# Two more buffers for expert weight pieces in a two-layer hybrid trunk step

## The reference

```python
for each layer l:
    sh1, sc1, g1, sh2, sc2, g2 = split(silu(cond) @ w_ada[l] + b_ada[l], 6)
    h = rms_norm(x, norm1) * (1 + sc1) + sh1
    qa, ka, va, hy, qr, kr, vr, gr = split(h @ w_in[l])        # 1024 x 4608
    ya = diff_attention(...)                                    # branch A
    yb = hyena_mixer(hy, ...)                                   # branch B, long convolution
    yc = retention(...) * silu(gr)                              # branch C
    ga, gb, gc = split(sigmoid(h @ w_gate[l] + b_gate[l]), 3)   # 1024 x 3072
    merged = ga * (ya @ w_branch_a) + gb * (yb @ w_branch_b) + gc * (yc @ w_branch_c)
    x = x + g1 * (merged @ w_out[l])
    h2 = rms_norm(x, norm2) * (1 + sc2) + sh2
    # 16 experts in 4 groups, best group, best 2 experts in it, for every token
    a = einsum('bld,edf->blef', h2, moe_w1[l]); b = einsum('bld,edf->blef', h2, moe_w3[l])
    x = x + g2 * einsum('blef,efd->bld', silu(a) * b * gate, moe_w2[l])
y = rms_norm(x, final_g)
```

## Time and profile before

| | us |
|---|---|
| median of the three runs | 1155.75 |
| profiled execution, span from first to last instruction | 1155.5 |
| PE busy | 1100.4 (95%) |
| PE weight load busy | 783.7 (68%) |
| DVE busy | 542.0 (47%) |
| ACT busy | 209.8 (18%) |
| POOL busy | 41.0 (4%) |

### The profile page before, as it was taken

One profiled execution on the slowest core, in us unless ns is written; L12 is line 12 of the kernel. 1 busy time (PEld: TensorE's weight loads), 2 busy tenths in 40 slices (PEclk: granted clock), 3 DMA queues, 4 the chain that ended last, 5 costly groups with the idle time before them and its releaser, 6 DMA issues.

```text
span 1155.5 us, 15668 instructions
## 1 busy us (share of the span) xinstructions
PE 1100.4 (95%) x6026; PEld 783.7 (68%) x6026; DVE 542.0 (47%) x1202; ACT 209.8 (18%) x440; POOL 41.0 (4%) x83
## 2 busy tenths in 40 slices
PE   6999999999999999999889999999999999999965
PEld 4688888878887445454358888888888844545422
DVE  2469887677846311121244886646543551111003
ACT  3251022232021101111025111323201210000001
POOL 1001110000000000000000111000000000000000
PEclk9999999999998999999999999999999899999999
DMA  9657865467587999999955677437347979999993
GB/s 382 284 204 279 326 221 227 168 270 272 219 350 318 419 420 422 420 421 421 421 219 201 215 276 285 174 133 283 139 145 306 375 305 421 421 420 421 421 420 121
DMA packets 56943, 351.38 MB, mean 304 GB/s; under 512 B 7088, under 2 KB 7264, under 8 KB 20512
## 3 DMA queue, kind: packets, MB, share of 16 engines
q1 hardware_dynamic: 52704, 337.75, 73.5%
q0 software_dynamic: 4160, 12.58, 3.0%
HBM read 346.08 MB, written 2.65 MB: 302 GB/s over the span
## 4 chain that ended last, share of the span: by engine, by line
PE 84%; DMA 8%; DVE 3%; SPq 3%; ACT 1%; issue 1%; DVEq 0%; ACTq 0%
PE bank L836 26%; PE bank L1127 15%; PE bank L1016 7%; PE bank L1148 6%; DMA ring<-in_experts 5%; PE bank L1037 5%; PE bank L831 5%; PE bank L1112 5%; PE bank L1169 3%; PE bank L847 3%; DMA ring<-in_weights 3%; SPq L615 2%; PE bank L760 1%; PE bank L820 1%; PE bank L961 1%
## 5 line engine op out<-in xcount | busy, mean ns | idle before, releaser
L836 PE MATMUL bank<-h,ring 128*128 128x256 f32 x1472 | 324.8, 380 | 0.0
L836 PEld LDWEIGHTS bank<-h,ring 128*128 128x128 f32 x1472 | 277.4, 190 | 40.1 <-issue 3.2
L1750 DVE SCALAR_TENSOR_TENSOR ring<-ring 128x1024 f32<-128x1024 f32 x160 | 189.5, 1222 | 18.7 <-DMA ring<-in_mod_weights 9.1
L1127 PE MATMUL bank<-ring,gates 128*32 128x512 f32 (+2 forms) x616 | 137.7, 614 | 8.8 <-DMA h<-in_experts 5.0
L1127 PEld LDWEIGHTS bank<-ring,gates 128*32 128x32 f32 (+2 forms) x616 | 41.2, 126 | 69.5 <-issue 69.1
L1127 PE MATMUL bank<-lent,gates 128*32 128x512 f32 (+2 forms) x408 | 81.4, 593 | 2.0 <-ACTq L1618 2.0
L2238 DVE COPY uc_zt_dsum<-bank 128x512 f32<-128x512 f32 x14 | 9.7, 692 | 122.8 <-PE bank L1148 122.8
L1148 PE MATMUL bank<-ring,gates 128*32 128x512 f32 (+1 forms) x240 | 64.4, 595 | 2.0 <-issue 1.2
L1148 PE MATMUL bank<-lent,gates 128*32 128x512 f32 (+2 forms) x304 | 60.5, 594 | 1.3 <-DMA ring<-in_experts 1.0
L1112 PE MATMUL bank<-uc_zt_dsum,gates 128*128 128x128 f32 x448 | 55.5, 285 | 1.0 <-DVEq L2246 1.0
L1127 PEld LDWEIGHTS bank<-lent,gates 128*32 128x32 f32 (+2 forms) x408 | 25.2, 123 | 46.2 <-issue 43.7
(11 more groups left out here) (271 smaller groups left out, 1203.7 us busy)
## 6 DMA issues: line engine op xcount, KB each, us to landing
ring<-in_experts SPq DMA_DIRECT2D x93, 1024.0 KB, 19.8
ring<-in_weights SPq DMA_DIRECT2D x85, 1024.0 KB, 7.7
lent<-in_experts SPq DMA_DIRECT2D x72, 1024.0 KB, 17.8
ring<-in_mod_weights SPq DMA_DIRECT2D x80, 512.0 KB, 5.1
h<-in_experts SPq DMA_DIRECT2D x10, 1024.0 KB, 19.4
uc_zt_dsum<-in_experts SPq DMA_DIRECT2D x10, 1024.0 KB, 19.5
va_vr<-in_experts SPq DMA_DIRECT2D x7, 1024.0 KB, 12.2
lent<-in_weights SPq DMA_DIRECT2D x3, 1024.0 KB, 23.5
```

The lines of the kernel that those rows point to most:

```text
L836: last = pe.matmul(bank[b][:, c * TOK:(c + 1) * TOK], w[:, k, c * P:(c + 1) * P], h[:, k, :], start=(k == 0), stop=(k == KT - 1))
L1127: last = pe.matmul(bank[b][rows, :], hgat[:, 4 * half + f, rows], w[j][:, f, :], start=(half == 1 and f == 0), stop=(half == 0 and f == 3) ...
L1750: last = dve.scalar_tensor_tensor(out, w, 0.5, cond_wide[:, c, :], ALU.mult, ALU.mult, accum_out=mod_all[:, of, row, c:c + 1])
```

## The change

ring_table gets two more slots for expert pieces. EXTRA_SLOT is a new tile of 128 x 2048 (8 KB per partition) that only expert pieces use, so it is open at any time. SPARE_SLOT is a tile of the same size, open once the merge is done; rinv, rmsi and condT become parts of it. The room comes from the scratch of GpSimd's queue, which shrinks from 16384 to 4096 bytes per partition, 12 KB, and from the three small tiles (4 KB per partition together), for two tiles of 8 KB. As every slot has a semaphore of its own, two are added and three others are joined to ones that exist: s_hid_sum to s_taps_sum, s_hid_arg to s_taps, s_taps_abs to s_hid, with the counts waited for adapted. The wait for the turned tokens (line 613) is confined to the three slots that need it.

```diff
@@ -85,6 +85,7 @@
 LANDINGS = 3
 TOKENS_SLOT = SLOTS + LENT
 SUMS_SLOT, SHIFT_SLOT = TOKENS_SLOT + 1, TOKENS_SLOT + 2
+EXTRA_SLOT, SPARE_SLOT = SHIFT_SLOT + 1, SHIFT_SLOT + 2
 SHIFT_PIECES = 36
 OPENING_LENT = (SLOTS, SLOTS + 1, SLOTS + 2)
 
@@ -149,7 +150,7 @@
     pieces = [(item, c) for item in PLAN for c in range(PLAN_PIECES[item[0]])]
     done = [(item, c) for item in DONE for c in range(PLAN_PIECES[item[0]])]
     gone = {piece: n + 1 for n, piece in enumerate(done)}
-    free, filled = [0] * (SHIFT_SLOT + 1), [0] * (SHIFT_SLOT + 1)
+    free, filled = [0] * (SPARE_SLOT + 1), [0] * (SPARE_SLOT + 1)
     slot, count, used = [], [], []
     for (kind, layer, number), c in pieces:
         since = {at: free[at] for at in range(LEAST)}
@@ -158,6 +159,8 @@
         elif kind == "moe":
             since.update({at: max(free[at], END["merge", layer, 5]) for at in range(LEAST, SLOTS + LENT)})
         if kind == "moe":
+            since[EXTRA_SLOT] = free[EXTRA_SLOT]
+            since[SPARE_SLOT] = max(free[SPARE_SLOT], END["merge", layer, 5])
             for at in (TOKENS_SLOT, SUMS_SLOT):
                 since[at] = max(free[at], END["out", layer, N_PROJ - 1])
             if layer == DEPTH - 1 or c < SHIFT_PIECES:
@@ -360,9 +363,7 @@
         s_h_ready_s = sem("h_ready_s")
         s_h_ready_v = sem("h_ready_v")
         s_h_scaled = sem("h_scaled")
-        s_hid = sem("hid")
-        s_hid_arg = sem("hid_arg")
-        s_hid_sum = sem("hid_sum")
+        s_hid = sem("hid_hid_taps_abs")
         s_idft_done = sem("idft_done")
         s_ktok_sum = sem("ktok_sum")
         s_kz_ready = sem("kz_ready")
@@ -412,13 +413,12 @@
         s_state_copied = sem("state_copied")
         s_state_sum = sem("state_sum")
         s_stored = sem("stored")
-        s_taps = sem("taps_decayed_scaled")
-        s_taps_abs = sem("taps_abs")
-        s_taps_sum = sem("taps_sum_norm")
+        s_taps = sem("arg_arg_taps_decayed_scaled")
+        s_taps_sum = sem("hid_hid_taps_sum_norm")
         s_va_copied = sem("va_copied")
         s_vector_link = sem("vector_link")
         s_vr_copied = sem("vr_copied")
-        s_weights_in = [sem(f"weights_in{slot}") for slot in range(SHIFT_SLOT + 1)]
+        s_weights_in = [sem(f"weights_in{slot}") for slot in range(SPARE_SLOT + 1)]
         s_weights_used = sem("weights_used")
         s_x_in = sem("x_in")
         s_x_mixed = sem("x_mixed")
@@ -463,6 +463,10 @@
                 return late[:, 8 * TOK:8 * TOK + PIECE]
             if SLOT[n] == SHIFT_SLOT:
                 return values[:, :]
+            if SLOT[n] == EXTRA_SLOT:
+                return extra[:, :]
+            if SLOT[n] == SPARE_SLOT:
+                return spares[:, :]
             return ring[:, SLOT[n], :] if SLOT[n] < SLOTS else lent[:, SLOT[n] - SLOTS, :]
 
         def part(slot, at, n):
@@ -490,15 +494,17 @@
         amix = part(3, 1024, 512).rearrange("p (a b) -> p a b", a=2)
         amixT = part(3, 1536, 512).rearrange("p (a b) -> p a b", a=2)
         osq = zt
-        rinv = sb("rinv", P, C_B)
+        extra = sb("extra", P, PIECE)
+        spares = sb("rinv_rmsi_condT", P, PIECE)
+        rinv = spares[:, 0:C_B]
         rms = tmp[:, 0:TOK]
         mod_row = rinv.rearrange("p (a b) -> p a b", a=2)
-        rmsi = sb("rmsi", P, TOK)
+        rmsi = spares[:, C_B:C_B + TOK]
         ones = sb("ones", P, P)
         modp = sb("modp", P, DEPTH, N_MODP)
         mod_all = sb("modT", P, DEPTH, 48, 2)
         amp_all = sb("amp", P, DEPTH, 2, 8, 2)
-        condT = sb("condT", P, 8, 32)
+        condT = spares[:, C_B + TOK:C_B + 2 * TOK].rearrange("p (a b) -> p a b", a=8)
         sm = sb("sm", P, 640)
         kz = probs[:, 0, :, :]
         swapped = [flat(probs[:, i, :, :]).rearrange("p (a b) -> p a b", a=4) for i in range(2)]
@@ -609,7 +615,7 @@
                 if SLOT[n] in range(LEAST, SLOTS) and not given[layer]:
                     sp.wait_ge(s_chunk_used, sum(CHUNKS[:layer + 1]))
                     given[layer] = True
-                if SLOT[n] >= TOKENS_SLOT and not turned[layer]:
+                if SLOT[n] in (TOKENS_SLOT, SUMS_SLOT, SHIFT_SLOT) and not turned[layer]:
                     sp.wait_ge(s_tokens_turned, 4 * (layer + 1))
                     turned[layer] = True
                 sp.dma_start(slot_of(n), source).then_inc(s_weights_in[SLOT[n]], 16)
@@ -782,30 +788,30 @@
                         pe.wait_ge(s_mod_params_in, 32)
                     take(4)
                     pe.matmul(bank[4][0:64, 0:128], R("f_w1", H_EMB), C("z", H_EMB), start=True,
-                              stop=True).then_inc(s_hid_sum, 1)
+                              stop=True).then_inc(s_taps_sum, 1)
                 elif n == 1:
-                    pe.wait_ge(s_hid, 2 * layer + 1)
+                    pe.wait_ge(s_hid, 3 * layer + 1)
                     take(4)
                     pe.matmul(bank[4][0:64, 0:128], R("f_w2", 64), hid[0:64, :], start=True,
-                              stop=True).then_inc(s_hid_sum, 1)
+                              stop=True).then_inc(s_taps_sum, 1)
                 elif n == 2:
                     pe.wait_ge(s_consts_in, 16)
                     pe.wait_ge(s_params_in, 16 * (layer + 1))
-                    pe.wait_ge(s_hid, 2 * layer + 2)
+                    pe.wait_ge(s_hid, 3 * layer + 2)
                     for c in range(2):
                         take(4 + c)
                         w3 = R("f_w3", 64)[:, c * 512:(c + 1) * 512]
                         pe.matmul(bank[4 + c][:, :], hid[0:64, :], w3, start=True,
                                   stop=True).then_inc(s_taps_sum, 1)
                 elif n == 3:
-                    pe.wait_ge(s_taps_abs, layer + 1)
+                    pe.wait_ge(s_hid, 3 * layer + 3)
                     take(4)
                     for c in range(2):
                         last = pe.matmul(bank[4][:, :], ones[:, :], habs[:, c, :], start=(c == 0),
                                          stop=(c == 1))
                     last.then_inc(s_taps_sum, 1)
                 else:
-                    pe.wait_ge(s_taps, 2 * layer + 2)
+                    pe.wait_ge(s_taps, 4 * layer + 4)
                     for b, a0, a1 in ((5, "cf", "cf1"), (6, "s0", "s1"), (7, "nq", "nq1")):
                         take(b)
                         pe.matmul(bank[b][:, :], C(a0), hs[:, 0, :], start=True, stop=False)
@@ -1344,12 +1350,12 @@
                 sc_e.sem_inc(s_bank_free[b], 1)
 
             def hid_sine(layer, n):
-                sc_e.wait_ge(s_hid_arg, 2 * layer + n + 1)
+                sc_e.wait_ge(s_taps, 4 * layer + n + 1)
                 sc_e.activation(hid[0:64, :], arg[0:64, :], ACT.Sin).then_inc(s_hid, 1)
 
             def taps_abs(layer):
-                sc_e.wait_ge(s_taps, 2 * layer + 1)
-                sc_e.activation(habs[:, :, :], hs[:, :, :], ACT.Abs).then_inc(s_taps_abs, 1)
+                sc_e.wait_ge(s_taps, 4 * layer + 3)
+                sc_e.activation(habs[:, :, :], hs[:, :, :], ACT.Abs).then_inc(s_hid, 1)
 
             def o_square(layer, j):
                 if j < 2:
@@ -1757,13 +1763,13 @@
 
             def taps_decay(layer):
                 for c in range(2):
-                    dve.wait_ge(s_taps_sum, 3 * layer + c + 1)
+                    dve.wait_ge(s_taps_sum, 5 * layer + c + 3)
                     link(tt(hs[:, c, :], bank[4 + c][:, :], C("decay"), ALU.mult))
                     dve.sem_inc(s_bank_free[4 + c], 1)
                 dve.sem_inc(s_taps, 1)
 
             def taps_scale(layer):
-                dve.wait_ge(s_taps_sum, 3 * layer + 3)
+                dve.wait_ge(s_taps_sum, 5 * layer + 5)
                 link(dve.reciprocal(tmp[:, :], bank[4][:, :]))
                 dve.sem_inc(s_bank_free[4], 1)
                 link(tt(hs[:, :, :], hs[:, :, :], tmp[:, :].unsqueeze(1).broadcast_to([P, 2, C_B]),
@@ -1772,7 +1778,7 @@
 
             def sine_arg(layer, n):
 
-                dve.wait_ge(s_hid_sum, 2 * layer + n + 1)
+                dve.wait_ge(s_taps_sum, 5 * layer + n + 1)
                 a, r = arg[0:64, :], rnd[0:64, :]
                 link(ts(a, bank[4][0:64, 0:128], R(f"f_b{n + 1}", 64), ALU.add))
                 dve.sem_inc(s_bank_free[4], 1)
@@ -1780,7 +1786,7 @@
                 link(ts(r, r, -ROUND, ALU.add))
                 link(stt(a, r, -TWO_PI_HI, a, ALU.mult, ALU.add))
                 link(stt(a, r, -TWO_PI_LO, a, ALU.mult, ALU.add))
-                ts(a, a, SIN_EDGE, ALU.min, -SIN_EDGE, ALU.max).then_inc(s_hid_arg, 1)
+                ts(a, a, SIN_EDGE, ALU.min, -SIN_EDGE, ALU.max).then_inc(s_taps, 1)
 
             dve.wait_ge(s_shared_in, 16)
             cond = H("cond").rearrange("p (a b) -> p a b", a=8)
@@ -2488,7 +2494,7 @@
     import concourse.bacc as _bacc
     from concourse.bass_utils import run_bass_kernel_spmd as _run
 
-    nc = _bacc.Bacc("TRN2", target_bir_lowering=False, num_devices=1)
```

(1 more changed line is left out.)

## The result

The changed kernel takes 1147.52 us, the median of 4 executions from 1145.75 to 1149.51; the kernel before, run beside it, 1155.69 (4 executions, 1154.02 to 1155.91). The ratio is 0.9927, with a 95% interval of 0.9914 to 0.9941: faster by 8.2 us. 1145.8 was forecast, range 1143.5 to 1151.0. The profiled execution took 1146.39 us, its span (first to last instruction) 1144.6.

The account below looks back on a forecast made before the run. The expert weight stream, up to piece 95's landing, was taken as the bound, with PE just ahead. Two pieces in each of two layers at 2.49 us gave 9.96 us: span 1155.5 to 1145.5, forecast 1145.8, range 1143.5 to 1151.0.

Parts of the forecast that it names:

- Two holes per layer: The expert weight stream idles before the merge's end and before its restart; each slot fills 2.49 us there per layer.
- The request into extra, the holes, the landing: Signs: piece 0 requested 0.4 us behind the last output-projection piece, second hole 2.5 us shorter, piece 95 landing at 573.2 and 1125.
- if a part of it doesn't fit: If piece 0 (2.49 us) overfills the first hole, it pushes the stream and still comes out of the second.
- Is something late next?: Behind the restart: register loads of about 2.1 us before piece 20 leave no bubble, as pieces 18 and 19 cover them.
- Rival (a): Register loads hold piece 20 after the restart, one piece per layer is lost: 1150.8; with partial fills, chance 0.15.
- Can PE follow?: In the expert stages PE's waits, 5.6 and 6.0 us, cover the 4.98 wanted, with 0.6 to spare in the first.
- rival (b): PE waits 2.3 us for piece 95; the last half runs at low clock, 1.7 us per layer: 1149.2, chance 0.08.
- Scratch 0, buffers and semaphores 0: GpSimd's 4096-byte scratch, moved buffers (-2 to +2 us, taken as 0) and joined semaphores cost nothing.
- The sum: Over both expert stages, 2 layers x 2 pieces x 2.49 = 9.96 us gained.
- the likeliest case: Whole kernel: the full 10 us gained, within 1144 to 1148, chance 0.66.
- The median stands 0.25 us above that span: Whole run: the median 1155.75 lies 0.25 us above the profiled span 1155.5, so 1145.5 became 1145.8.

Follow-up runs that it names:

- the two kernels with thin pieces: Changed kernel with two pieces per stage loaded to a sixteenth only: 2 and 3, ahead of the restart, ratio 0.9925; 30 and 31, behind it, 0.9858.
- Moving the loads: Changed kernel with item 2's three register loads on SyncE moved from before piece 20 to before piece 18: 1146.61 us, ratio 0.9914.

## Why the prediction was right, and where its sizes were off

**"Two holes per layer" and each slot worth a piece: right, by a little less.** 2.49 us per slot and layer were forecast; the stages got 4.84 and 4.79 us shorter for 4.98, together 9.6 us for 9.96, and 15 to 18 slots give 2.5 us each. That the pieces behind the restart, and not the bytes ahead of it, carry the gain is shown by the two kernels with thin pieces: 0 and 6.6 us.

**The request into extra, the holes, the landing: as forecast,** the first hole taking a part of its piece only: 1.7 us of 2.49 in layer 0 and 1.1 in layer 1; the rest came out of the second, as "if a part of it doesn't fit" had it. Piece 95 landed at 572.6 and 1123.9; 573.2 and 1125 were forecast.

**"Is something late next?": no, as forecast.** The restart still hangs on PE: at 373.65 for 374.14, and at 924.68 for 930.92, where 5.3 us come from layer 0 and about 0.9 from the routing ahead of it, told of below. Moving the loads changed nothing. Rival (a), half the gain, falls.

**"Can PE follow?": yes, and with as little to spare as forecast.** Of the 5.6 us of waits in the first layer 2.25 are left, which is the prediction's 5.6 + 1.7 - 4.98 = 2.3. It had these 2.3 us in rival (b), with the price of a fallen clock at 1.7 us, but put them in front of the last half. They stand in front of the second half of item 5's out-product, at piece 89, which the prediction named as late for a quicker PE without following it. Rival (b) holds there, in part of the executions and in layer 0 alone: of eight profiles with 18 slots in that layer (the one with thin pieces behind the restart aside) three show the fallen clock and a stage of 204.7 to 204.9 us, five do not and show 202.9 to 203.2. The waits ahead of it were 2.43, 2.47 and 2.63 us in the three, 2.03 to 2.44 in the five, and with EXTRA_SLOT alone the clock fell behind 2.29 us. So in these executions PE could not follow by the whole gain in layer 0. The Trainium skill ("TensorE: Matmul & The Clock Gate", What's actually happening) has a monitor lower the clock by how busy PE has lately been; that the clock falls behind a wait agrees (0.79 over 556:562 behind 2.43 us). Why nearly equal waits end differently, no run here settles.

For the second layer the prediction counted 5.0 + 1.0 = 6.0 us of waits. That sum was too small: its own have 2.2 us more, and two of 0.3 and 1.2 us belong to it, the second put down to "issue" though its piece, 89, asked for at 1092.27, landed 27.8 us later, at 1120.1, and the product followed at 1120.15. That makes 9.7 us. Therefore a third slot and the thin pieces still shortened the stage of layer 1, by 2.3 and 3.6 to 3.8 us.

**Scratch 0, buffers and semaphores 0: right,** 1.0001 [0.9988, 1.0014] for all of them.

**The sum: 10.0 us forecast, 8.2 measured, 9.6 in the stages.** One term was a little too large: the slots brought 4.84 + 4.79 for 4.98 + 4.98, which is 0.3 us less. And one is missing: some executions lose 1.7 us in layer 0 to the clock, which the likeliest case had at nothing. The rest is scatter: against the kernel before of their own group the three runs of the change gained 8.2, 9.2 and 10.3 us by the medians.

**"The median stands 0.25 us above that span": a wrong reading that did no harm.** The prediction took the profiled execution for a median one. In the four executions after, the time is 1.8, 1.8, 2.0 and 2.0 us more than the span. By that, the profiled execution of before took about 1157.4 us and was 1.7 above its median. As the 10.0 us were taken off the median in effect, the sum did not suffer; a comparison of spans does. Of their 10.9 us, 9.6 are the stages. The opening of the profiled execution after was 1.63 us earlier and gave 1.1 back in the routing; and the stretch between the stages was 0.9 us longer in the kernel before, where PE ran with a granted clock of 0.50 over 920 to 924, just ahead of the second stage, and of 1.00 over 914 to 918 after. Neither belongs to the change. The kernel with neither slot has the early opening too, and the two repetitions of the change ask for the last output-projection piece at 314.90 and 314.73, as late as the kernel before; between the stages they took 347.93 and 349.26 us, with the same program.

## What to carry to other kernels

Where a stream is busy at its full rate nearly always, as here, a slot more is worth about one piece of its time (2.3 to 2.6 us for 2.49) in each stage in which the stream stands for want of a slot; look for the idle stretch ahead of the stream's restart, not at its average, and leave the bytes ahead of it out of the account. Sum all waits of the engine behind it in the stage, with those that the view puts down to "issue" but a landing ends: they are the limit. The next wait can lie at another piece than the last, and a lower clock behind it takes a part of the gain back (1.7 us here). Take the offset between a span and a run's time from several executions, never from one.

## What the runs showed of the hardware

- In layer 0 a wait of 2.3 to 2.6 us on PE is followed by the lower clock in some executions (2.29, 2.43, 2.47, 2.57, 2.63 us) and not in others (2.25, 2.32, 2.44, 2.54), and what decides was not found. Behind the waits of 3.65 to 3.84 us in layer 1, six profiles with 18 slots have 32 products in 4.97 to 5.17 us, where at full clock they take 3.64. Yet a longer wait need not be followed by it: with neither slot, PE waited 3.81 us and its next 32 products took 3.64 us, as at full clock, while in the kernel before 32 products after the same 3.81 us took 5.34:

```profile
548.90 3.64 PE L1131 MATMUL bank<-ring,gates 128*32 128x512 f32 x32 [3.81 <-DMA ring<-in_experts]
```

- With 1024 bytes of scratch GpSimd stood 4.38 and 7.48 us after four of eight copies of 32 KB, in two of six groups. With 4096 bytes five of the six went out without a pause, and the sixth had pauses of 0.7 and 0.3 us.
- The last expert pieces of a stage take 26 to 31 us from request to landing, though one moves in 2.49 us: ten to a dozen stand in the queue, an estimate from these two numbers. Requests then hold SyncE for about 2 us each, where a request takes 0.33 us otherwise.
